# A transformer block on one core: the norm of the differential output takes four steps instead of three, and the other norms of a turn start a step later

## What is computed

```python
h = rms_norm(x, norm_mix)
proj = h @ w_in                        # q, k, v of two mixers, forget logits
# mixer A, 8 heads: two 64-wide q/k maps each, RMS-normed, ALiBi, block-causal mask
p  = probs(q1, k1) - lam * probs(q2, k2)
oa = rms_norm(p @ v, subln_diff) * (1.0 - lambda_init)
# mixer B, 8 heads of 128: q and k RMS-normed, log-forget-gate bias, causal mask
ob = forgetting_attention(qb, kb, vb, log_f_cum)
gates  = sigmoid(h @ w_gate + b_gate)
merged = g_diff * (oa @ w_branch_diff) + g_fox * (ob @ w_branch_fox)
x = x + merged @ w_out
x = x + relu(rms_norm(x, norm_mlp) @ w_mlp_up) ** 2 @ w_mlp_down
```

## Time and profile before

| | |
|---|---|
| median of 3 runs | 2800.96 us (2799.61 to 2801.01) |
| the profiled execution | 2801.55 us, of which the span 2799.8 us |
| PE busy over the span | 2726.6 us (97%) |
| DVE, ACT busy | 1754.5 us (63%), 1160.1 us (41%) |
| PE share of the chain that ended last | 88% (DVE 6%, issue 3%, ACT 2%) |
| heads stage, 477 to 1120 us: PE, DVE, ACT busy | 592.82, 443.60, 269.05 us of 643 |

### The profile page before, as it was taken

One profiled execution on the slowest core, in us unless ns is written; L12 is line 12 of the kernel. 1 busy time (PEld: TensorE's weight loads), 2 busy tenths in 40 slices (PEclk: granted clock), 3 DMA queues, 4 the chain that ended last, 5 costly groups with the idle time before them and its releaser, 6 DMA issues.

```text
span 2799.8 us, 44340 instructions
## 1 busy us (share of the span) xinstructions
PE 2726.6 (97%) x15942; PEld 2410.6 (86%) x15942; DVE 1754.5 (63%) x3065; ACT 1160.1 (41%) x1563; POOL 36.0 (1%) x60
## 2 busy tenths in 40 slices
PE   8999999999999999999999999999999999999999
PEld 7999999777777778888889999999998888888887
DVE  4548887677777775443468787878774444454544
ACT  5534443444444344223344444444444343434333
POOL 0000000000000000000000000000000000000000
PEclk9999999999999999999999999999999999999999
DMA  7334444322222224444333434343447565666653
GB/s 249 108 119 128 135 127 120 90 68 68 67 63 67 68 68 129 142 143 143 121 128 128 135 127 135 122 135 126 135 130 253 194 226 187 198 216 201 218 197 118
DMA packets 359586, 387.20 MB, mean 138 GB/s; under 512 B 16448, under 2 KB 273984, under 8 KB 358976
## 3 DMA queue, kind: packets, MB, share of 16 engines
q1 hardware_dynamic: 331920, 347.24, 39.6%
q10 hardware_dynamic: 27568, 38.81, 3.9%
HBM read 348.23 MB, written 37.75 MB: 138 GB/s over the span
## 4 chain that ended last, share of the span: by engine, by line
PE 88%; DVE 6%; issue 3%; ACT 2%; DMA 1%; SPq 0%; DVEq 0%; ACTq 0%
PE job L1671 5%; PE job L1674 5%; PE job L1673 5%; PE scores L1974 2%; PE job L1974 2%; PE job L1978 2%; PE job L1976 2%; PE scores L1978 2%; PE scores L1976 2%; PE job L2001 2%; PE job L2003 2%; PE job L2002 2%; PE scores L2001 2%; PE scores L2002 2%; PE scores L2003 2%
## 5 line engine op out<-in xcount | busy, mean ns | idle before, releaser
L1608 DVE TENSOR_TENSOR w_lo_d<-raw_d,w_hi_d 128x512 fp32r<-128x512 f32 x256 | 176.2, 690 | 368.9 <-ACT w_hi_d L1031 368.9
L1347 DVE TENSOR_TENSOR lo<-pair,hi 128x1792 fp32r<-128x1792 f32 x142 | 287.1, 2022 | 125.2 <-ACT hi L809 125.2
L809 ACT ACTIVATE hi<-pair 128x1792 fp32r<-128x1792 f32 x142 | 241.5, 1700 | 272.3 <-PE heads_out L1978 118.7
L665 ACT ACTIVATE w_hi<-raw 128x512 fp32r<-128x512 f32 x272 | 171.0, 631 | 386.9 <-PE job L1674 268.5
L1031 ACT ACTIVATE w_hi_d<-raw_d 128x512 fp32r<-128x512 f32 x256 | 161.5, 632 | 405.5 <-PE heads_out L2003 202.8
L1086 DVE TENSOR_TENSOR w_lo<-raw,w_hi 128x512 fp32r<-128x512 f32 x272 | 188.9, 696 | 176.4 <-ACT w_hi L665 170.6
L1671 PE MATMUL job<-a_hi,w_hi 128*128 128x512 f32 x576 | 239.4, 416 | 2.9 <-DVE w_lo L1086 2.9
L1674 PE MATMUL job<-a_hi,w_lo 128*128 128x512 f32 x576 | 228.6, 397 | 0.0
L1673 PE MATMUL job<-a_lo,w_hi 128*128 128x512 f32 x576 | 227.9, 396 | 0.0
L1974 PE MATMUL scores<-h,hi 128*128 128x256 f32 x512 | 145.4, 284 | 4.7 <-DVE h L1540 2.6
L1614 DVE TENSOR_TENSOR u_lo<-u_raw,u_hi 128x2048 fp32r<-128x2048 f32 x64 | 146.2, 2284 | 4.5 <-ACT u_hi L1037 4.5
(11 more groups left out here) (449 smaller groups left out, 7782.4 us busy)
## 6 DMA issues: line engine op xcount, KB each, us to landing
pair<-in_w_mlp_up SPq DMA_DIRECT2D x256, 256.0 KB, 2.8
u_raw<-u_rows SPq DMA_DIRECT2D x64, 1024.0 KB, 5.6
raw_d<-in_w_mlp_down SPq DMA_DIRECT2D x128, 512.0 KB, 6.2
raw<-in_w_in SPq DMA_DIRECT2D x80, 512.0 KB, 4.1
pair<-in_w_gate SPq DMA_DIRECT2D x84, 256.0 KB, 2.9
raw<-in_w_out SPq DMA_DIRECT2D x64, 256.0 KB, 3.3
u_rows<-u_out ACTq DMA_DIRECT2D x32, 512.0 KB, 4.3
raw<-in_w_in SPq DMA_DIRECT2D x24, 344.0 KB, 3.2
```

What stands on the lines that cost most here:

```text
L665: nc.scalar.activation(w_hi[:, u % SPLITS], raw[:, slot, part:part + KU], ACT.Copy).then_inc(hi_ready, 1)
L809: nc.scalar.activation(pair_hi[j % 2], pairs[j][:, :, 1:8], ACT.Copy).then_inc(pair_hi_ready, 1)
L1347: nc.vector.tensor_tensor(pair_lo[j % 2], pairs[j][:, :, 1:8], pair_hi[j % 2].bitcast(F32), ALU.subtract).then_inc(pair_lo_ready, 1)
L1608: nc.vector.tensor_tensor(w_lo_d[:, j % SPLITS], raw_d[:, j // 2, j % 2], w_hi_d[:, j % SPLITS].bitcast(F32), ALU.subtract).then_inc(down_ ...
```

## The change

`NORM_STEPS` moves w0k0 from t = 4 to 5 and the norms of a forgetting head from (6, 9) to (7, 10); w1k0 (8) and w2 (27) start where they did. `NORM_LENGTH` becomes a table: w2 takes four steps, its `widen` comes at u = 15 instead of 14, all others stay at three. The low part of the differential output is no longer at the front of DVE's step 15 but at its very end, behind `split_unit`; the forgetting head's stays at u = 15 and waits for one rounding less, since ACT now rounds that output first. The merge waits for both low parts at once.

```diff
-NORM_STEPS = ((4, 8, 27), (6, 9))
-NORM_LENGTH = 3
+NORM_STEPS = ((5, 8, 27), (7, 10))
+NORM_LENGTHS = ((3, 3, 4), (3, 3))
...
-                if kind == 0 and t == NORM_STEPS[0][2] + NORM_LENGTH:
+                if kind == 0 and t == NORM_STEPS[0][2] + NORM_LENGTHS[0][2]:
                     act.wait_ge(norm_ready, norm_no(0, 2, i) + 1)
                     nc.scalar.activation(tile(b_hi, i), v_feat, ACT.Copy).then_inc(o_hi, 1)
...
                 if kind == 1 and t == 23:
-                    dve.wait_ge(o_hi, i * 2 + 2)
+                    dve.wait_ge(o_hi, i * 2 + 1)
                     nc.vector.tensor_tensor(tile(b_lo, i + H), heads_out[:, :], tile(b_hi, i + H).bitcast(F32),
                                             ALU.subtract).then_inc(o_ready, 1)
-                if kind == 0 and t == NORM_STEPS[0][2] + NORM_LENGTH + 1:
-                    dve.wait_ge(o_hi, i * 2 + 1)
-                    nc.vector.tensor_tensor(tile(b_lo, i), v_feat, tile(b_hi, i).bitcast(F32),
-                                            ALU.subtract).then_inc(o_ready, 1)
...
                 if kind == 0 and t == NORM_STEPS[0][2] + 1:
                     invert_rms(norm_no(0, 2, i), r_wide, HD)
+                if kind == 0 and t == NORM_STEPS[0][2] + NORM_LENGTHS[0][2]:
+                    dve.wait_ge(o_hi, i * 2 + 2)
+                    nc.vector.tensor_tensor(tile(b_lo, i), v_feat, tile(b_hi, i).bitcast(F32),
+                                            ALU.subtract).then_inc(o_ready, 1)
...
-            def norm_steps(n, t, first):
+            def norm_steps(kind, which, i, t):
+                n, first = norm_no(kind, which, i), NORM_STEPS[kind][which]
                 if t == first + 1:
                     pe.wait_ge(sq_ready, n + 1)
                     turn_squares(n, squares)
-                if t == first + NORM_LENGTH:
+                if t == first + NORM_LENGTHS[kind][which]:
                     widen(n, r_wide)
...
                 if first:
                     pe.wait_ge(tail_scaled, 3)
-                    pe.wait_ge(o_ready, 2 * H - 1)
+                    pe.wait_ge(o_ready, 2 * H)
```

More of the change, by code:

```diff
@@ L704, in norm_step @@
                 for which in range(2 if kind == 0 else 0):
-                    if t == NORM_STEPS[0][which] + NORM_LENGTH:
+                    if t == NORM_STEPS[0][which] + NORM_LENGTHS[0][which]:
                         act.wait_ge(norm_ready, norm_no(0, which, i) + 1)
@@ L1223, in scale_step @@
                 for which, result in enumerate((qk_normed, qk_normed) if kind == 0 else (qn_fox, kn_fox)):
-                    if t == NORM_STEPS[kind][which] + NORM_LENGTH:
+                    if t == NORM_STEPS[kind][which] + NORM_LENGTHS[kind][which]:
                         scale_by_rms(norm_no(kind, which, i), result)
-                if kind == 0 and t == NORM_STEPS[0][2] + NORM_LENGTH:
+                if kind == 0 and t == NORM_STEPS[0][2] + NORM_LENGTHS[0][2]:
                     scale_by_rms(norm_no(0, 2, i), v_feat)
@@ L1231, in split_step @@
                 for which in range(2 if kind == 0 else 0):
-                    if t == NORM_STEPS[0][which] + NORM_LENGTH + 1:
+                    if t == NORM_STEPS[0][which] + NORM_LENGTHS[0][which] + 1:
                         dve.wait_ge(qk_hi, i * 2 + which + 1)
@@ L1732, in head_step @@
                 for which in range(2):
-                    norm_steps(norm_no(kind, which, i), t, NORM_STEPS[kind][which])
+                    norm_steps(kind, which, i, t)
                 if kind == 1 and t == BIAS_STEP:
@@ L1768, in head_step @@
                 if kind == 0:
-                    norm_steps(norm_no(0, 2, i), t, NORM_STEPS[0][2])
+                    norm_steps(0, 2, i, t)
             def value_unit(q, k):
@@ L1911, in merge @@
                     pe.wait_ge(tail_scaled, 4)
-                    pe.wait_ge(o_ready, 2 * H)
                 else:
```

## The result

| | before | after |
|---|---|---|
| median | 2800.87 us (2799.61 to 2801.01, 4 runs) | 2781.39 us (2780.71 to 2782.59, 4 runs) |
| the profiled execution, its span | 2801.55, 2799.8 us | 2782.59, 2780.8 us |

The ratio is 0.9931 (95% interval 0.9919 to 0.9943): 19.5 us faster.

The account below looks back on a forecast made before the run. PE, busy for 97% of the span, was taken as the bound. Six turns entered by the branch gave -9.0 us, the first turn -1.4, the tail about 0: -10.4 on 2801.55, so 2791.1, taken as 2791, range 2785 to 2802.

Parts of the forecast that it names:

- The next turn's first instruction 3.0 us later, at X+6.65: DVE's loop branch at X+3.65, next turn starting 3.0 us later; X is the start of step 15 on PE.
- Step 1: PE's wait for DVE's copy of block 0 falls to 0.55 us, saving 2.25, plus 1.6 of slow clock, six times.
- Step 2: New PE wait of 1.6 us ahead of `widen` for w0k1's inverse root, in six turns.
- Steps 8 to 11: The differential q's low part delays block 2's probabilities: a new PE wait of 0.7 us in each of seven turns.
- 0.60 - 0.90 + 0.36 = +0.06 us: Step 14, per turn: PE restarts 0.60 later, `widen` at half speed (0.90) leaves and costs 0.36 at full speed.
- B: Rival: PE's clock falls at the new wait of step 2, 1.6 us back six times, 2800.6 us; chance 0.15.
- A: Rival: DVE's branch isn't reached early, first instruction at X+7.45, 4.8 us less gain, 2796 us; chance 0.13.
- C: Rival: slow clock lasts behind step 2's wait, +1.0 us six times, 2807; chance 0.12 including other unseen waits.
- a stall at step 0: PE standing for ACT's `scaled` of w0k1; forecast as no cost, done by X+3.35, PE asking at X+3.6.
- D: Rival: DVE makes up steps 9 to 11's 0.7 us, or step 2's wait is shorter, seven turns, 2786; chance 0.08.

Follow-up runs that it names:

- after + 16: The changed kernel with 16 one-column memsets added to DVE's program in the values stage, loop at places 426 to 721; 2797.52 us, ratio 0.999.
- before + 48: The kernel before the change with 48 one-column memsets added to DVE's program, loop at places 473 to 769; 2779.03 us, ratio 0.9921.
- shift only: The kernel before with NORM_STEPS alone changed to ((5, 8, 27), (7, 10)), w2 still three steps long; 2779.52 us, ratio 0.9918.
- root in step 13: The changed kernel with w2's inverse root moved from DVE's step 12 to the end of step 13, behind the copy of block 3; 2742.12 us, ratio 0.979.
- both edits: The kernel "root in step 13" with the low part of the differential q in DVE's step 10 instead of 9; 2736.54 us, ratio 0.9772.
- both edits + 16: The kernel "both edits" with 16 memsets added to DVE's program, loop at places 426 to 721; 2749.9 us, ratio 0.9814.
- after + 64: The changed kernel with 64 memsets added to DVE's program, loop at places 474 to 769; 2782.25 us, ratio 0.9932.
- after + 40: The changed kernel with 40 memsets added to DVE's program, loop at places 450 to 745; 2783.4 us, one run.
- after + 2: The changed kernel with 2 memsets added to DVE's program, loop at places 412 to 707; 2800.28 us, one run.
- after + 8: The changed kernel with 8 memsets added to DVE's program, loop at places 418 to 713; 2801.61 us, one run.
- after + 38: The changed kernel with 38 memsets added to DVE's program, loop at places 448 to 743; 2812.63 us, one run.
- root in step 13, w2 at three steps: The kernel "shift only" with w2's inverse root moved to DVE's step 13; 2783.12 us, ratio 0.9934.

## Why the prediction was right and wrong

All profiled executions together allow a sum. The waits are PE's listed ones in the heads stage (without the two kinds that every kernel has alike), the slow clock is counted as above and costs half of its length; what is left of the span should be the same everywhere.

| kernel | span | waits | slow clock | span - waits - half of slow |
|---|---|---|---|---|
| before | 2799.8 | 46.1 | 58.0 | 2724.7 |
| after | 2780.8 | 39.1 | 30.7 | 2726.4 |
| after + 16 | 2794.8 | 50.1 | 41.0 | 2724.2 |
| before + 48 | 2778.6 | 34.7 | 34.1 | 2726.9 |
| shift only | 2778.2 | 32.4 | 47.8 | 2721.9 |
| root in step 13 | 2740.4 | 12.1 | 0.0 | 2728.3 |
| both edits | 2734.0 | 9.3 | 0.0 | 2724.7 |
| both edits + 16 | 2749.5 | 20.5 | 0.0 | 2729.0 |
| after + 64 | 2780.2 | 39.4 | 23.9 | 2728.9 |
| after + 40 | 2781.7 | 39.6 | 27.3 | 2728.5 |
| after + 2 | 2798.6 | 56.3 | 44.4 | 2720.1 |
| after + 8 | 2799.9 | 53.4 | 47.8 | 2722.6 |
| after + 38 | 2810.9 | 57.4 | 51.2 | 2727.9 |
| root in step 13, w2 at three steps | 2780.6 | 43.1 | 23.9 | 2725.6 |

The spans differ by 77 us and what is left by 9, from 2720.1 to 2729.0. So waits and the clock behind them are the account but for a few us, and a difference of 2 to 5 us between two kernels can't be read from it.

- **"The next turn's first instruction 3.0 us later, at X+6.65": this step failed.** The branch came at X+3.63 as forecast, and the instruction at X+4.98. I had read the 3.0 us as the price of a taken branch; it is that of a fetch, which the place of the loop decides. Against the run that keeps my assumption (2797.5) it is worth 16.1 us of the 19.5: 11.0 in waits and 5.2 in slow clock, all of the latter behind step 14, where no run shows what the jump has to do with it. I had used the rule of the Trainium skill on fetches ("Runtime: NRT & Kernel Launch", Instruction fetch mechanics) to say when the gap starts, and not to ask whether the loop's start would still lie outside the blocks held.
- **The trace of before could have warned.** The branch of another loop of DVE, line 1408, 67 instructions long, is followed by the sequencer's next row 0.2 us later:

```profile
L1408 DVEq COMPARE_BRANCH  x1: 63/63/63, 270.4 to 270.4; - x1
L1408 DVEq FUSED_REGOPS  x1: 63/63/63, 270.6 to 270.6; - x1
```

The same holds for every other branch of DVE outside the heads stage that is taken: the next row comes 0.2 to 0.3 us behind it.

- **Step 1.** With the jump as assumed, the six waits are 2.3 us in all, 0.4 each (forecast 0.55), and the 20.5 us of slow clock behind them go, 10.2 us of time (forecast 9.6). Right.
- **Step 2.** 1.75 us with the slow jump (forecast 1.6); 0.3 to 0.4 with the quick one, since the root starts that much earlier.
- **Steps 8 to 11.** 5.0 us in seven waits (forecast 4.9). Right.
- **"0.60 - 0.90 + 0.36 = +0.06 us" at step 14: the term was mis-sized.** The wait grew by 0.6 as said. But I took back 0.5 us a turn because `widen` no longer runs at half speed. Whatever stands behind the wait runs slow instead, for 3.4 or 6.8 us in each turn. Behind step 14 that was 37.5 us before and 41.0 in after + 16, so +1.7 us where I had -3.8. These 5.5 us, and 1.0 us more of waits than forecast, are most of the 6.4 us between 2791.1 and 2797.5. But the size of this term is not settled by one kernel: in the same order the slow clock is 41.0 to 47.8 us with 2, 8 and 16 memsets, and 23.9 to 30.7 with none, 40 and 64.
- **Rivals.** B, the clock falling at step 2, did not happen in any run. A, C and a stall at step 0 did not either: the branch was early. D's mechanism (shorter waits) is what came, from a source that I had not named.

So the change of order itself is worth little, and its sign isn't clear. At the slow places it brought 3 us with 16 memsets (2800.65 to 2797.52, an interval that just leaves out 1), but next to nothing in the single runs with 2 and 8 (2800.28 against 2801.97, 2801.61 against 2801.79). At the quick places it cost 3 us (before + 48 has 2779.03, after + 64 has 2782.25; their runs don't overlap, the intervals of their ratios do). The gain of 19.5 us comes from DVE's loop having moved by 15 places. That the time fell clearly, as forecast, is luck: the move of the loop stood nowhere in my sum.

What stays open: why a slow stretch lasts 3.4 us in one turn and 6.8 in the next of the same kernel, and why the long ones are more frequent with the slow jump in the new order; and why the limits lie at 450 and 706 and not at multiples of 256, which some 62 instructions ahead of the listed ones would explain, though no run shows them.

## To carry to other kernels

When a loop's edge shows an idle gap that nothing releases, look at the queue of fetched instructions on the page and at the edges of the engine's other loops before you take the gap for the price of a branch. The loop of 295 instructions here jumped in 0.3 us or in 3, by its place alone, so a change that adds or removes a few instructions ahead of it must be costed for that, and a gain must be checked with a few idle instructions added. And where a step of slack is given to a chain, see that the instruction which makes the bottleneck wait is moved with it: the slack alone brought nothing here, and with the move 39 us.

## What the hardware showed

The slow jump costs DVE's sequencer 2.8 to 3.1 us in most kernels here, 3.5 to 3.7 where the branch stands just behind the limit (2 memsets), and 3.0 + 2.6 us where the start lies just short of one (38). The quick jump costs 0.3 us. Waits of PE of 1.75 us left the granted clock at 1.00, and so did one of 2.44 us (in the kernel with the moved root and w2 at three steps) and one of 2.55 (after + 38); all those of 2.66 to 5.04 us were followed by 3.4 or 6.8 us at 0.50. In the three kernels where no wait of PE in the stage was over 1.8 us, the clock was full throughout.
